# Modulation vectors in whole-vector loads, eight expert weight slots, and a first norm applied after the transpose, in a two-layer hybrid MoE step

## The chip, the cores and the metric

The kernel runs on one core of one Trainium2 chip. Five engines work side by side, each with its own instruction queue: TensorE (PE: matmuls, and transposes done as matmuls), VectorE (DVE), ScalarE (ACT), GpSimd (POOL) and SyncE (SP), which here does nothing but issue DMAs. Semaphores, written out by hand, order them. The metric is the device time of one execution in microseconds; lower is better. All data are FP32.

## The reference

A step of a two-layer backbone (D = 1024), run for 128 prompt tokens with the conditioning `c_ctx` and for 256 latent tokens with `c`:

```python
def modulation(cvec, w_mod_l, b_mod_l):
    m = jax.nn.silu(cvec) @ w_mod_l + b_mod_l
    return m.reshape(cvec.shape[0], 6, D_MODEL)

def trunk_layer(x, mod, ...):
    sh1, sc1, g1, sh2, sc2, g2 = [mod[:, i][:, None, :] for i in range(6)]
    h = rms_norm(x, n1) * (1.0 + sc1) + sh1
    proj = h @ w_in
    q, k, v, u = jnp.split(proj, [Q_W, Q_W + KV_W, Q_W + 2 * KV_W], axis=-1)
    ...                                   # QK-norm, rotary (latent only), softmax attention
    conv = conv_module(u, dw_w, dw_b, ln_g, ln_b)      # 31-tap depthwise convolution
    x = x + g1 * (jnp.concatenate([attn, conv], axis=-1) @ w_out)
    h2 = rms_norm(x, n2) * (1.0 + sc2) + sh2
    x = x + g2 * grouped_moe(h2, w_router, b_router, wg, wu, wd)
    return x, k, v
```

`grouped_moe` sends each token to 2 of 16 experts. An expert is `silu(t @ w_gate) * (t @ w_up)` and then `@ w_down`, each matrix 1024 x 512 or 512 x 1024, 2.1 MB. The weights of a layer (101 MB in the experts, 25 MB for modulation, 11.5 MB in the projections) are read once.

## The kernel before

The 384 tokens are three tiles of 128 (tile 0 the prompt, tiles 1 and 2 the latents), and both conditionings run together: the two cond vectors stand side by side in `cs_rep`, and every modulation product gives rows for both. Tokens stay in `x`.

**Weights.** `ring` has six slots (`SLOTS`) of 16 KB per partition, one per 2.1 MB matrix. Loads are numbered items; item n uses slot n % 6, and SyncE issues them strictly in order, each waiting for `slot_used` of the item six before. A modulation vector of 1024 columns is two items, chunks of 512 columns (`MODC` = 12 chunks a layer, vectors 0 to 5: shift, scale, gate of the first half, then of the second). The order in a layer is: chunks 4 and 5, the four parts of `w_in`, chunks 6 to 9, the two halves of `w_out`, chunks 10 and 11, the next layer's chunks 0 to 3, and then the experts, `g1 u1 d0 g2 u2 d1` and so on. In layer 0 chunks 0 to 3 come first of all.

**Modulation** (`modulation`, line 1277). For a chunk with lanes, TensorE keeps 64 columns of weights (`cs_rep[:, k]`, the two vectors repeated) on each half of the array: the left half streams columns 0 to 255 of the chunk, the right half columns 256 to 511, both at once (line 1294). Chunks 8 and 9, the fifth vector, have no lanes: two columns of weights and 512 streamed (line 1291). VectorE adds the bias (`mod_take`, line 854); for a scale vector it also forms (1 + scale) times the norm's gain. The rows then go to DRAM and come back spread over all partitions (`lane_out` and `spread` on GpSimd) into `shiftB`, `scaleB`, `gateB`. The first ones, of layer 0, are broadcast by TensorE instead (line 1313) and copied out by ScalarE and VectorE.

**Before the experts.** ScalarE squares and sums each tile, GpSimd forms the reciprocal root, and VectorE makes `h` in two passes over 1024 columns (`norm`, lines 907 and 909). TensorE transposes `h` (line 1333), ScalarE copies to `hT`, and 12 projections follow in the order `PROJ` (line 1272). VectorE runs the 31 convolution taps (line 943) between its other duties: the prompt's during the projections; for the latents 6 beside the rotary work, 4 (16 instructions) before the first head, and 3 (12 instructions) in each of the first seven heads. TensorE's modulation work is filler: chunks 6 and 7 around the transposes of q and k, and a quarter of chunk 8 or 9 in each of the 8 heads (`HEAD_FILL`). In a head, VectorE finds the row maxima (line 1023), ScalarE the exponentials, TensorE transposes them, starts the next head's scores, runs the filler and multiplies with v. Then come the output projection (line 1482), the second norm, the router, VectorE's selection, and chunks 10, 11 and the next layer's 0 to 3 as filler.

**Experts** (`expert`, line 1601). GpSimd gathers 128 rows, 64 for each of two experts. TensorE transposes them (line 1552), then per expert: gate and up (line 1568, 16 products of 512 columns on array halves), the down product of the expert before (line 1584), transposes of the hidden rows. An expert with more than 64 tokens has further passes through `overflow`, with their own gather, gate/up and down. `slot_used` of gate and up is raised by tiny products at the very end of the expert (line 1598). At the end of a layer GpSimd gathers the stored expert rows, and `combine` adds them to `x`.

## Time and profile before

| | us |
|---|---|
| median of 3 runs | 1209.04 |
| lowest, highest | 1206.81, 1209.96 |
| the profiled execution | 1206.56 |
| its span, first to last instruction | 1204.7 |

| engine | busy us | share of the span |
|---|---|---|
| TensorE | 995.3 | 83% |
| VectorE | 417.0 | 35% |
| ScalarE | 158.1 | 13% |
| GpSimd | 118.8 | 10% |

The core moves 333.79 MB, 277 GB/s over the span. In the profile the engines are PE, DVE, ACT, POOL and SP; PEld is TensorE's weight load, which overlaps, and a name with q (SPq) is an engine's queue. Each FP32 product that isn't a transpose leaves two records, so "x32" is 16 products. The granted clock of TensorE is a share of 2.4 GHz; 0.5 is the lower of its two levels. The stages of the execution, in us: layer 0 before its experts 0 to 312, its experts 312 to 595, layer 1 before its experts 595 to 875, its experts 875 to 1178, the last combine to the end.

### The profile page before, as it was taken

The numbers are of one execution on the slowest core, as the hardware profiler recorded it, in microseconds if no ns is written. First come the engines' busy times: TensorE is split into PE (matmuls) and PEld (weight loads), VectorE is DVE, ScalarE is ACT, GpSimd is POOL, SyncE is SP. The second block draws the span as 40 slices with busy tenths as digits, with TensorE's granted clock in tenths as the row PEclk, the third lists the DMA queues.
The fourth block names the chain that finished last, engine by engine and source line by source line (L and its number), as shares of the span: only waits on it lengthen the run. The fifth ranks groups of instructions, "written<-read, shape, count | busy, mean of one in ns | idle before, by whom it ended". The sixth has DMA issues, their size and how long they took to land.

```text
span 1204.7 us, 11958 instructions
## 1 busy us (share of the span) xinstructions
PE 995.3 (83%) x4410; PEld 465.3 (39%) x4410; DVE 417.0 (35%) x1070; ACT 158.1 (13%) x354; POOL 118.8 (10%) x164
## 2 busy tenths in 40 slices
PE   3799989998879988888819998999688788788891
PEld 2544545556323333333314554555432223323330
DVE  0229879445111111111051987934410111101113
ACT  0110134220000000000021014422000000000001
POOL 0010300511100000000031030051110000000001
PEclk8899979998889999988858997999688889988996
DMA  9984971387899777999985442135666997999825
GB/s 298 390 294 155 229 267 70 101 241 301 349 420 423 304 308 284 427 426 425 402 299 178 140 159 91 35 122 208 256 237 245 424 424 298 399 427 425 341 88 174
DMA packets 78410, 333.79 MB, mean 277 GB/s; under 512 B 6461, under 2 KB 10685, under 8 KB 61925
## 3 DMA queue, kind: packets, MB, share of 16 engines
q1 hardware_dynamic: 56528, 277.89, 58.2%
q0 software_dynamic: 9104, 30.79, 7.2%
q10 hardware_dynamic: 12676, 23.76, 6.8%
q8 instruction: 64, 1.05, 0.3%
q14 instruction: 38, 0.30, 0.1%
HBM read 310.31 MB, written 22.10 MB: 276 GB/s over the span
## 4 chain that ended last, share of the span: by engine, by line
PE 59%; DMA 22%; DVE 11%; SPq 3%; issue 2%; ACT 2%; POOL 1%; ACTq 0%; DVEq 0%; POOLq 0%
PE ps L1568 17%; PE ps L1272 15%; DMA ring<-in_w_up_dram 14%; PE ps L1584 8%; PE ps L1482 7%; DVE scr L943 4%; DMA ring<-in_w_down_dram 4%; PE ps L1294 3%; DMA scr<-h_rows,slot_tok 2%; PE ps L1407 2%; PE ps L1552 2%; DMA ring<-in_w_mod_dram 2%; SPq L364 1%; DMA scr<-expert_rows,pick_y 1%; PE ps L1291 1%
## 5 line engine op out<-in xcount | busy, mean ns | idle before, releaser
L1568 PE MATMUL ps<-ring,hT 128*64 128x512 f32 x1024 | 257.5, 661 | 52.6 <-DMA ring<-in_w_up_dram 40.3
L1568 PEld LDWEIGHTS ps<-ring,hT 128*64 128x64 f32 x1024 | 83.9, 152 | 201.6 <-issue 187.7
L943 DVE SCALAR_TENSOR_TENSOR scr<-scr,convw 128x128 f32<-128x128 f32 (+1 forms) x480 | 160.7, 415 | 0.0
L1584 PE MATMUL ps<-ring,scr 128*64 128x512 f32 x624 | 144.7, 605 | 5.8 <-DVE scr L1235 3.0
L1272 PE MATMUL ps<-ring,hT 128*128 128x512 f32 (+1 forms) x384 | 147.5, 545 | 0.0
L1244 DVE TENSOR_TENSOR scr<-ps,scr 128x256 f32<-128x256 f32 x32 | 13.6, 425 | 351.3 <-ACT scr L831 351.3
L1294 PE MATMUL ps<-ring,cs_rep 128*64 128x256 f32 x640 | 91.5, 447 | 25.9 <-DMA ring<-in_w_mod_dram 25.9
L1272 PEld LDWEIGHTS ps<-ring,hT 128*128 128x128 f32 x384 | 73.4, 192 | 70.7 <-issue 68.4
L1482 PE MATMUL ps<-ring,hT 128*128 128x512 f32 x192 | 84.4, 594 | 1.3 <-ACT hT L698 1.3
L1584 PEld LDWEIGHTS ps<-ring,scr 128*64 128x64 f32 x624 | 48.8, 139 | 89.8 <-issue 85.4
L1294 PEld LDWEIGHTS ps<-ring,cs_rep 128*64 128x64 f32 x640 | 51.6, 161 | 60.7 <-issue 26.6
L831 ACT ACTIVATE scr<-ps 128x256 f32<-128x256 f32 x32 | 12.3, 383 | 400.0 <-PE ps L1568 400.0
L1568 PE MATMUL ps<-ring,scr 128*64 128x512 f32 x224 | 53.0, 629 | 5.9 <-DVE scr L1224 5.9
L1482 PEld LDWEIGHTS ps<-ring,hT 128*128 128x128 f32 x192 | 35.7, 190 | 43.0 <-issue 41.1
L565 POOL DMA_INDIRECT scr<-h_rows,slot_tok x16 | 15.5, 967 | 317.2 <-PE ps L1552 272.9
L1333 PE MATMUL ps<-table_sb,h 128*128 128x128 f32 x96 | 17.6, 341 | 29.4 <-DVE h L909 29.4
L1216 DVE COPY hT<-ps 128x512 f32<-128x512 f32 x32 | 20.6, 686 | 56.8 <-PE ps L1552 56.8
L1407 PE MATMUL ps<-scr 64*128 64x384 f32 (+1 forms) x96 | 39.4, 500 | 0.0
L1291 PE MATMUL ps<-ring,cs_rep 128*2 128x512 f32 x64 | 32.6, 636 | 0.0
L1552 PE MATMUL ps<-table_sb,scr 128*128 128x128 f32 x128 | 20.1, 305 | 14.8 <-DMA scr<-h_rows,slot_tok 14.8
L1272 PEld LDWEIGHTS ps<-scr 128*128 128x128 f32 x224 | 26.2, 191 | 15.2 <-issue 13.0
L799 ACT COPY scr<-ps 128x512 f32<-128x512 f32 x32 | 18.7, 585 | 100.4 <-PE ps L1584 100.4
(196 smaller groups left out, 770.2 us busy)
## 6 DMA issues: line engine op xcount, KB each, us to landing
ring<-in_w_gate_dram SPq DMA_DIRECT2D x32, 2048.0 KB, 11.5
ring<-in_w_up_dram SPq DMA_DIRECT2D x32, 2048.0 KB, 16.2
ring<-in_w_down_dram SPq DMA_DIRECT2D x32, 2048.0 KB, 20.9
ring<-in_w_mod_dram SPq DMA_DIRECT2D x22, 2048.0 KB, 8.8
ring<-in_w_in_dram SPq DMA_DIRECT2D x6, 2048.0 KB, 19.7
expert_rows<-scr ACTq DMA_DIRECT2D x78, 128.0 KB, 7.6
ring<-in_w_out_dram SPq DMA_DIRECT2D x4, 2048.0 KB, 14.8
expert_rows<-x ACTq DMA_DIRECT2D x1, 6656.0 KB, 36.3
```

The lines of the kernel that those rows point to most:

```text
L799: a.copy(ybuf[:, j, :], ps[:, YB + j, :]).then_inc(y_taken, 1)
L943: v.scalar_tensor_tensor(out, span, w, out, ALU.mult, ALU.add).then_inc(conv_step[part_], 1)
L1216: ins = v.tensor_copy(hT[:, i % 2, 4 * b:4 * b + 4, :].rearrange("p k n -> p (k n)"), ps[:, XT + b, :])
L1272: mm = pe.matmul(out, stationary(k), moving(k), start=(k == 0), stop=(k == n - 1))
L1291: mm = pe.matmul(ps[0:2, mod_bank(l, c), :], cs_rep[:, k, 0:2], w, start=(k == 0), stop=(k == KD - 1))
L1294: mm = pe.matmul(ps[b * LP:(b + 1) * LP, mod_bank(l, c), 0:LW], cs_rep[:, k, :], w[:, b * LW:(b + 1) * LW], start=(k == 0), stop=(k == KD ...
L1333: mm = pe.transpose(ps[:, n % 4, m * P:(m + 1) * P], h[:, t, k::KD], ident)
L1407: pe.matmul(ps[:, 4 + t, 0:P * len(ks)], qT[g_ * HD:(g_ + 1) * HD, t, j * P:(j + 1) * P], kT[g_ * HD:(g_ + 1) * HD, ks[0] * P:(ks[-1] + 1) ...
L1482: mm = pe.matmul(ps[:, out_bank(t, n), :], hT[:, t, k, :], slot_w(s)[:, k, :], start=(k == 0), stop=(k == KD - 1))
L1552: mm = pe.transpose(ps[:, XT + m // 4, m % 4 * P:(m % 4 + 1) * P], xs[:, i % 2, m::KD], ident)
L1568: mm = pe.matmul(ps[b * TT:(b + 1) * TT, bank, :].rearrange("p (m n) -> p m n", m=2), tokens(k), w[:, :, k, b * HF:(b + 1) * HF], start=(k ...
L1584: mm = pe.matmul(ps[b * TT:(b + 1) * TT, bank, :], src[:, k % 2 * P + k // 2 * TT:k % 2 * P + (k // 2 + 1) * TT], w[:, k, b * SEG:(b + 1) ...
```

## The change

**Vectors, not chunks.** An item is now half of a vector's contraction rows, all 1024 columns (4 KB runs in DRAM in place of 2 KB). The left half of the array streams columns 0 to 511, the right half columns 512 to 1023. The fifth vector is done so too. One `mod_take` takes a whole vector, so it needs the vector's last product. In layer 0 the third vector moves from before the projections to behind them. A head's filler is one contraction row of vector 4 (2 products of 512 columns, one on each array half).

**Eight places.** `place()` assigns slots ahead of time by running the order of releases through a list of free slots. Slots 6 and 7 are new for the experts only: slot 6 is the memory of `shiftB` and `scaleB`, free when the second norm is done, slot 7 that of `h` and one tile of `hT`, free when `h` is stored and the router has read. SyncE's loop over the experts is written out.

**The first norm.** VectorE writes only a diagonal matrix with the tile's reciprocal roots (`scale_tile`). TensorE multiplies `x` with it, which scales and transposes at once. ScalarE and VectorE apply scale and shift on the way out of PSUM, four 128-column blocks each per tile, from `modcol`, in which scale and shift are columns. These come through DRAM (`columns`): on ScalarE's queue for layer 0, on GpSimd's for layer 1. The broadcast by TensorE, the copies and the first `spread` pair of layer 1 are gone.

```diff
+def loads(l):
+
+    vec = [("v", l, j, b) for j in range(6) for b in range(2)]
+    proj, out = [("in", l, m) for m in range(4)], [("out", l, n) for n in range(2)]
+    if l == 0:
+        items = vec[0:4] + proj + vec[4:10] + out + vec[10:12]
+    else:
+        items = vec[4:6] + proj + vec[6:10] + out + vec[10:12]
+    if l + 1 < LAYERS:
+        items += [("v", l + 1, j, b) for j in range(2) for b in range(2)]
+    experts = [("g", l, 0), ("u", l, 0)]
+    for e in range(1, E):
+        experts += [("g", l, e), ("u", l, e), ("d", l, e - 1)]
+    return items, experts + [("d", l, E - 1)]
...
+def place():
...
+        at = next((n for n, s in enumerate(free) if s < limit), None)
+        while at is None:
+            done = order.pop(0)
+            free.extend((SLOTS, SLOTS + 1) if done == "norm" else (slot[done],))
+            at = next((n for n, s in enumerate(free) if s < limit), None)
+        slot[item] = free.pop(at)
+        count[slot[item]] += 1
+        use[item] = count[slot[item]]
...
         gateB = sb("gateB", [P, 2, D])
-        h = sb("h", [P, TILES, D])
-        hT = sb("hT", [P, TILES, KD, P])
+        h = ring[:, SLOTS + 1, 0:TILES * D].rearrange("p (t n) -> p t n", n=D)
+        at_hT = ((SLOTS + 1) * KD * SEG + TILES * D)
+        hT = [big[:, at_hT + t * D:at_hT + (t + 1) * D].rearrange("p (k n) -> p k n", k=KD) for t in (2, 1, 0)]
...
+        diag = h[:, :, 0:P]
...
+        def columns(eng, l):
+
+            eng.wait_ge(mod_done, 2 * l + 1)
+            lane_out(eng, mod_dram[:, 0:2 * D], rowA, modA_st[l])
+            eng.wait_ge(modA_st[l], 32)
+            for g_ in range(2):
+                eng.dma_start(modcol[:, g_], mod_dram[g_, 0:2 * D].rearrange("(s p k) -> p s k", s=2, k=KD))\
+                    .then_inc(modcol_in[l], 16)
+
...
-                    load_mod(l, c_)
+                if l:
+                    load_vector(l, 2)
 
                 for m, (c0, n) in enumerate(((QW + 2 * KVW + CH, CH), (QW + 2 * KVW, CH), (0, QW), (QW, 2 * KVW))):
                     if l and m == 2:
                         sp.wait_ge(combined, (l - 1) * TILES + 2)
-                    load(IN_AT[l] + m, w_in_v[l, :, :, c0:c0 + n], n)
-                for c_ in range(MODN, MOD2):
-                    load_mod(l, c_)
+                    load(("in", l, m), w_in_v[l, :, :, c0:c0 + n], n)
+                for j in (2, 3, 4) if l == 0 else (3, 4):
+                    load_vector(l, j)
...
+                def slot_free(n):
+
...
+                    if s >= SLOTS and uses(n) - 1 == (BORROWED[l - 1] if l else 0):
+                        if s == SLOTS:
+                            sp.wait_ge(h_ready, l * 3 + 3)
+                        else:
+                            sp.wait_ge(h2_st, (l + 1) * (TILES * 16))
+                            sp.wait_ge(logit_ps, l * 3 + 3)
+                    elif past(uses(n) - 1):
+                        sp.wait_ge(slot_used[s], uses(n) - 1)
+                    return s
...
                 if l == 0:
-
-                    for n in range(4):
-                        act.wait_ge(first_bc_ps, n + 1)
-                        a.copy(scaleB[:, n // 2, n % 2 * SEG:(n % 2 + 1) * SEG], ps[:, 4 + (n + 1) % 4, :]).then_inc(first_scale, 1)
-                for t in range(TILES):
-                    take_hT(0, t)
+                    columns(act, 0)
+                act.wait_ge(modcol_in[l], 32)
+                for t in range(TILES):
+                    act.wait_ge(hT_ps, l * 18 + 2 * t + 1)
+                    for m in range(4):
+                        ins = a.activation(hT[t][:, m, :], ps[:, 2 * t % 4, m * P:(m + 1) * P], ACT.Identity,
+                                           bias=modcol[:, group(t), 0, m:m + 1], scale=modcol[:, group(t), 1, m:m + 1])
+                    ins.then_inc(hTa_ready, 1)
...
+                def scale_tile(t):
+
+                    dve.wait_ge(rstd_ready, l * 6 + t + 1)
+                    v.tensor_scalar(diag[:, t, :], ident, stats(R1 + t), None, ALU.mult).then_inc(diag_ready, 1)
+
+                def take_hT(t):
+
+                    dve.wait_ge(modcol_in[l], 32)
+                    dve.wait_ge(hT_ps, l * 18 + 2 * t + 2)
+                    for m in range(4):
+                        k = 4 + m
+                        ins = v.tensor_scalar(hT[t][:, k, :], ps[:, (2 * t + 1) % 4, m * P:(m + 1) * P],
+                                              modcol[:, group(t), 1, k:k + 1], modcol[:, group(t), 0, k:k + 1],
+                                              ALU.mult, ALU.add)
+                    ins.then_inc(hTd_ready, 1)
...
+                    scale_tile(0)
                     combine(l - 1, 2)
-                norm(0, 1)
-                norm(0, 2)
+                else:
+                    scale_tile(0)
+                scale_tile(1)
+                scale_tile(2)
                 if l == 0:
-                    mod_take(l, MOD1 + 1)
+                    mod_take(0, 1)
+                for t in range(TILES):
...
+                if l == 0:
+                    mod_take(l, 2)
+                mod_take(l, 3)
                 for k in range(LATE_TAPS):
                     tap(1, ROPE_TAPS + k)
...
-                    if HEAD_FILL[hd][2] == KD:
-                        mod_take(l, HEAD_FILL[hd][0])
+                    if hd == HEADS - 1:
+                        mod_take(l, 4)
...
+            def vector(l, j, k0=0, k1=KD):
+
+                for n, a, b in pieces(l, j):
...
+                        w = slot_k(slot_of(n), b - a)[:, k - a, :]
+                        for lane in range(LANES):
+                            mm = pe.matmul(ps[lane * LP:(lane + 1) * LP, mod_bank(l, j), :], cs_rep[:, k, :],
+                                           w[:, lane * LW:(lane + 1) * LW], start=(k == 0), stop=(k == KD - 1))
+                        if k == b - 1:
+                            mm.then_inc(slot_used[slot_of(n)], 1)
...
+                for t in range(TILES):
+                    pe.wait_ge(diag_ready, l * 3 + t + 1)
+                    if t == 2:
+                        hT_first(0)
+                    for n in range(2 * t, 2 * t + 2):
+                        for m in range(4):
+                            mm = pe.matmul(ps[:, n % 4, m * P:(m + 1) * P], x[:, t, 4 * (n % 2) + m::KD], diag[:, t, :],
+                                           start=True, stop=True)
+                        mm.then_inc(hT_ps, 1)
 
...
-                modulation(l, MODN, 0, KD // 2)
+                if l == 0:
+                    vector(l, 2)
+                vector(l, 3, 0, 2)
...
                     if t == 2:
                         mm.then_inc(qkT_ps, 1)
-                    c, k0 = ((MODN, KD // 2), (MODN + 1, 0), (MODN + 1, KD // 2))[t]
-                    modulation(l, c, k0, k0 + KD // 2)
+                    vector(l, 3, 2 * t + 2, 2 * t + 4)
...
-                    c, k0, k1 = HEAD_FILL[hd]
-                    if k0 == 0 and c > 8:
-                        pe.wait_ge(mod_taken, l * MODC + c)
-                    modulation(l, c, k0, k1)
+                    if hd == 0:
+                        pe.wait_ge(mod_taken, taken_at(l, 3))
+                    vector(l, 4, hd, hd + 1)
```

On TensorE, in layer 0 between the last projection and the first head (1395 or 1421 are the transposes of q and k), before:

```order
L1272 MATMUL ps<-ring,hT 128x256 x8
L1294 MATMUL ps<-ring,cs_rep 64x256 x8
L1391 MATMUL ps<-table_sb,scr 128x128
L1395 MATMUL ps<-table_sb,h 128x128 x4
L1397 MATMUL ps<-table_sb,scr 128x128
L1294 MATMUL ps<-ring,cs_rep 64x256 x8
```

and in the changed kernel:

```order
L1314 MATMUL ps<-big 128x256 x8
L1330 MATMUL ps<-big,cs_rep 64x512 x20
L1417 MATMUL ps<-table_sb,scr 128x128
L1421 MATMUL ps<-table_sb,big 128x128 x4
L1423 MATMUL ps<-table_sb,scr 128x128
L1330 MATMUL ps<-big,cs_rep 64x512 x4
```

16 products of 512 columns, the third vector, and the fourth's first four now stand ahead of the transposes. On VectorE, from the end of the last tile's rotary work to the maxima of the first head, before:

```order
L1008 TENSOR_TENSOR scr<-scr 128x128
L872 TENSOR_TENSOR scaleB<-ps,scaleB 128x256
L943 SCALAR_TENSOR_TENSOR scr<-scr,convw 128x256 x16
L872 TENSOR_TENSOR scaleB<-ps,scaleB 128x256
L1023 TENSOR_REDUCE stat<-ps 128x1 x3
```

and in the changed kernel (`big` is the memory of the slots, here the fourth vector's row):

```order
L1052 TENSOR_TENSOR scr<-scr 128x128
L906 TENSOR_TENSOR rowC<-ps,rowC 128x512
L906 TENSOR_TENSOR big<-ps,big 128x512
L987 SCALAR_TENSOR_TENSOR scr<-scr,convw 128x256 x16
L1068 TENSOR_REDUCE stat<-ps 128x1 x3
```

The second take moved from behind the 16 taps to ahead of them. On SyncE, with the semaphore that each issue waits for, from layer 0's first expert load, before (the last rows are in a loop):

```order
L413 DMA ring<-in_w_gate_dram 128x4096 [waits slot_used4]
L413 DMA ring<-in_w_up_dram 128x4096 [waits slot_used5]
L413 DMA ring<-in_w_gate_dram 128x4096 [waits slot_used0]
L413 DMA ring<-in_w_up_dram 128x4096 [waits slot_used1]
L421 DMA ring<-in_w_down_dram 128x2x2048 [waits slot_used2]
```

and in the changed kernel:

```order
L462 DMA big<-in_w_gate_dram 128x4096 [waits h_ready]
L462 DMA big<-in_w_up_dram 128x4096 [waits logit_ps,h2_st]
L462 DMA big<-in_w_gate_dram 128x4096 [waits slot_used4]
L462 DMA big<-in_w_up_dram 128x4096 [waits slot_used5]
L467 DMA big<-in_w_down_dram 128x2x2048 [waits slot_used0]
L462 DMA big<-in_w_gate_dram 128x4096 [waits slot_used1]
L462 DMA big<-in_w_up_dram 128x4096 [waits slot_used2]
L467 DMA big<-in_w_down_dram 128x2x2048 [waits slot_used3]
```

The first expert's two matrices no longer wait for the slots of chunks 10 and 11, and each later load of this stage stands two slots earlier in the course of the filler.

## Rows read from the trace of the kernel before

**Rows 1.** The page, part 4: shares of the span by line in the chain.
```profile
PE ps L1568 17%; PE ps L1272 15%; DMA ring<-in_w_up_dram 14%; PE ps L1584 8%; PE ps L1482 7%; DVE scr L943 4%; DMA ring<-in_w_down_dram 4%; PE ps L1294 3%; DMA scr<-h_rows,slot_tok 2%; PE ps L1407 2%; PE ps L1552 2%; DMA ring<-in_w_mod_dram 2%; SPq L364 1%; DMA scr<-expert_rows,pick_y 1%; PE ps L1291 1%
```

**Rows 2.** Windows: start:end length, engines' busy us (instructions), TensorE clock, DMA share, GB/s.
```profile
312.50:595.20 282.70, 238.98 (x1102) 90.94 (x1104) 34.57 (x74) 17.82 (x37) 10.82 (x13) 0.92 0.92 376
875.40:1178.00 302.60, 254.30 (x1160) 94.55 (x1160) 36.44 (x78) 18.78 (x39) 9.49 (x10) 0.91 0.81 330
390.00:480.00 90.00, 79.36 (x378) 30.14 (x374) 12.60 (x27) 6.78 (x14) 2.81 (x3) 0.96 0.74 299
870.00:930.00 60.00, 48.31 (x226) 19.25 (x228) 8.18 (x17) 3.29 (x7) 3.69 (x4) 0.90 0.62 229
930.00:990.00 60.00, 50.53 (x226) 18.29 (x223) 7.49 (x16) 3.87 (x8) 2.81 (x3) 0.88 1.01 426
990.00:1050.00 60.00, 49.98 (x242) 19.73 (x242) 6.74 (x15) 3.87 (x8) 0.97 (x2) 0.94 0.84 348
```

**Rows 3.** Waits of the whole span: who waited for whom, us, times, longest.
```profile
PE ps L1568 <- DMA ring<-in_w_up_dram: 40.3, 13, 6.8
...
PE ps L1598 <- issue: 18.0, 6, 4.0
```

**Rows 4.** Timeline of TensorE, experts: start, us, instructions, idle time before and its releaser.
```profile
354.84 9.97 PE L1568 MATMUL ps<-ring,hT 128*64 128x512 f32 x32 [6.77 <-DMA ring<-in_w_up_dram]
...
455.18 7.09 PE L1568 MATMUL ps<-ring,scr 128*64 128x512 f32 x32 [0.93 <-DVE scr L1224]
...
1102.85 9.73 PE L1568 MATMUL ps<-ring,hT 128*64 128x512 f32 x32 [0.54 <-DMA ring<-in_w_up_dram]
```

**Rows 5.** Timeline of the SyncE queue, third expert's loads in layer 0.
```profile
311.21 0.35 SPq L413 DMA_DIRECT2D ring<-in_w_gate_dram  x1
321.70 0.34 SPq L413 DMA_DIRECT2D ring<-in_w_up_dram  x1
```

**Rows 6.** Heads of layer 0: window of one head, then its modulation products.
```profile
184.86:191.54 6.68, 6.68 (x34) 3.46 (x33) 6.41 (x19) 2.81 (x9) 0.00 (x0) 1.00 0.03 3
...
188.12 1.88 PE L1291 MATMUL ps<-ring,cs_rep 128*2 128x512 f32 x4
```

**Rows 7.** Timeline of TensorE at the start of layer 0.
```profile
30.72 3.67 PE L1294 MATMUL ps<-ring,cs_rep 128*64 128x256 f32 x32 [0.43 <-DMA ring<-in_w_mod_dram]
36.39 5.36 PE L1294 MATMUL ps<-ring,cs_rep 128*64 128x256 f32 x32 [2.00 <-DMA ring<-in_w_mod_dram]
...
67.58 12.61 PE L1272 MATMUL ps<-ring,hT 128*128 128x512 f32 x29
```

**Rows 8.** Timeline around the entry to layer 0's heads.
```profile
141.93 1.95 PE L1294 MATMUL ps<-ring,cs_rep 128*64 128x256 f32 x16
...
151.69 0.66 PE L1395 MATMUL ps<-table_sb,h 128*128 128x128 f32 x4 [2.56 <-DVE scr L1008]
151.89 6.42 DVE L943 SCALAR_TENSOR_TENSOR scr<-scr,convw 128x256 f32<-128x256 f32 x16
...
152.39 3.63 PE L1294 MATMUL ps<-ring,cs_rep 128*64 128x256 f32 x16
...
158.55 1.22 DVE L1023 TENSOR_REDUCE stat<-ps 128x1 f32<-128x128 f32 x3
```

**Rows 9.** DMA issues (KB each, median us to landing), and a timeline row.
```profile
scr<-in_b_mod_dram ACTq DMA_DIRECT2D x4, 256.0 KB, 8.2
...
mod_rows<-rowC POOLq DMA_DIRECT2D x4, 4.0 KB, 5.5
...
310.06 0.75 POOL L472 DMA_DIRECT2D gateB<-mod_rows  x1 [14.27 <-DMA mod_rows<-scaleB]
```

**Rows 10.** Timeline of the first norm of layer 1.
```profile
622.43 1.28 DVE L907 SCALAR_TENSOR_TENSOR h<-x,stat,scaleB 128x1024 f32<-128x1024 f32 x1 [0.74 <-POOL stat L468]
...
623.75 1.23 DVE L909 TENSOR_TENSOR h<-h,shiftB 128x1024 f32<-128x1024 f32 x1
...
634.46 1.97 PE L1333 MATMUL ps<-table_sb,h 128*128 128x128 f32 x8 [1.29 <-DVE h L909]
```

467 lines of the change are left out of this document (201 added, 266 removed).

## The prediction

> **What bounds the kernel now.** I read the page first: the chain of work that ended last is mostly TensorE matmuls, led by the experts' gate and up products (line 1568), but `w_up` transfers hold a large second share [rows 1]. So I asked for the stages. The reader is to see in the windows of the two expert phases that TensorE is busy for 239 of 283 us and for 254 of 303 us, and that the DMA engines run in two regimes: 426 GB/s where they are full, and 299, 229 and 348 GB/s where they are not [rows 2]. Both engines idle, in turn, in one phase: the signature of a buffer that is too short. The waits say how much of it TensorE pays, both layers together: 40.3 us for `w_up`, and 18.0 us of stops at the small products that end an expert [rows 3]. The timeline shows the cause. The 16 gate/up products of an expert take 7.09 us. After 6.77 us of waiting the same products take 9.97 us, because the granted clock has dropped, so a wait costs up to 2.9 us more than itself; there are eleven such slow sets, the last at 1102.85. An expert with more than 64 tokens runs everything twice (such a second pass starts at 455.18), another 7.1 us and a down product during which its slots stay occupied [rows 4]. The SyncE queue shows the other side: `g2` leaves at 311.21, `u2` only at 321.70, when expert 0 has finished [rows 5]. Six slots are two experts of lookahead.
>
> Before the experts, each layer is bound by TensorE or by short chains; the loads of layer 0's first two vectors bound the first 50 us.
>
> **The change part by part.** All times are against the profiled execution, 1206.56 us with a span of 1204.7; the median of the three runs shown is 1209.04, 2.5 us higher.
>
> *Eight places for expert weights.* A 2.097 MB load takes 4.92 us at 426 GB/s [rows 2], so two more places hold 9.8 us of transfer per stretch in which the DMA would otherwise stop. The placement lets gate and up of an expert wait for the expert three back, not two, and lets `g0` go as soon as the second norm is done.
> - Layer 0: the gap is 90 us at 299 GB/s, or 90 x (1 - 299/426) = 26.8 us of DMA idleness, spread over three experts with a second pass, 8.9 us each, under the 9.8 that two places cover. The last experts still wait a little, since transfers (some 5.4 us per load with the row stores and gathers beside it) are slower than a plain expert's 12 us per three loads. I take -24.
> - Layer 1: 60 us at 229 GB/s is 27.7 us idle, 60 us at 348 is 11.0. The first gap is the ring standing full before expert 0 and during expert 1's second pass: two places fill 9.8, and one more load of 4.9 can go in the second pass because `d2` no longer queues behind `g3`. The second gap gives its 9.8. Sum -24.5. The two experts with second passes at the end are TensorE's own time and stay.
> - Bounds: TensorE can't get back more than it loses. In both layers that is 40.3 + 18.0 us of waits and 27.0 us that the eleven slow sets took above 7.09 each, 85.3 in all [rows 3, 4]; at the other end it gets nothing.
>
> *The heads' fifth vector on column halves.* Two products of 512 columns with 2-column weights take 1.88 us a head [rows 6]; as two halves side by side they should take half, since a chunk of 16 products with 256 columns takes 3.67 us [rows 7], which is 4 x 0.92. So TensorE falls from 6.68 to 5.74 us a head. But VectorE is busy 6.41 us of those 6.68 [rows 6]: the gain in a middle head is at most 0.27 us, 1.7 over six heads, not 5.6. The first head runs at half clock and is TensorE's, so it gives 1.6.
>
> The Trainium skill, page "TensorEngine Tiling (Array Packing)", Key Properties, says that changing the tiling mode drains TensorE, which speaks against putting half-array products between full-array ones in each head. The trace shows 8 products of that kind ahead of full-array work in 1.95 us, against 3.67 for 16 in a row [rows 7, 8]: at most 0.12 us for the switch. With it or without it, VectorE hides it; the sum is the same.
>
> *What VectorE now waits for.* This is the part that costs. Before, the fourth vector was taken in two chunks: the first was ready when the rotary work ended, then 16 taps ran (6.42 us), and the second chunk had arrived under them [rows 8]. Now `mod_take(l, 3)` stands ahead of the taps and needs the whole vector, whose last quarter TensorE computes after the transposes of tile 2, which wait for the same rotary work. Behind it on VectorE are 16 taps and then the first head's maxima, for which ScalarE and TensorE wait. In layer 1: transposes 0.76, fill 3.6 at half clock, take 0.7, taps 6.42, so the maxima come 11.5 us after the rotary end instead of 6.9: +4.6 (+2.8 at full clock). In layer 0 the third vector (7.3 us) is put in front too. TensorE starts its fills at 141.93, then 7.3 + 1.8, and three times transposes 0.9 and fill 1.8: 159.1. Take, taps: maxima at 166.3, not 158.55 [rows 8]: +7.7. From this come off head 0 (1.6), the middle heads (1.7) and about 2 us that TensorE had as slack behind the last tap. Net +3 in layer 0, 0 in layer 1; range 0 to +7.7 and -2 to +4.6.
>
> *Start of layer 0.* Removed: the broadcast products, the copies and two passes of the norm; and the fifth and sixth chunk move behind the projections. Added: a trip through DRAM, mod row out and column in, then the affine on the way out of PSUM. The second vector is complete at about 41.8, as before: its last products start at 36.39 and take 5.36 us [rows 7], but VectorE first scales three diagonals, so the row is done at 46. Two small stores with weights streaming beside them took 5.5 us; a store of the same sort took 14.3 in the worst wait [rows 9]. Reading 512 pieces of 32 bytes is not in the trace; the nearest are 8.2 us for 64 x 4 pieces of 1 KB per transfer, and 5.5 for a few rows. I take 8.2. With some 2 us for four issues: columns at 62. Then tile 0's affine (1.1), tile 2's products, which wait for tile 0's banks (3.4 at half clock), and the first projection at 66.5 instead of 67.58 [rows 7]; 1.2 lost to the clock leaves 0. From -5 (both trips at 5.5 us) to +9 (a 14.3 us store).
>
> *First norm of layer 1.* Here the columns are there long before. VectorE's two passes (1.28 + 1.22) become one pass over 128 columns, an eighth of the width and about 0.2 us [rows 10]. Ahead of tile 2's products lie tile 0's and tile 2's passes: -4.6. The products with a diagonal are true FP32 products: 3.4 us for 8 at half clock against 1.97 for transposes [rows 10]: +1.4. Net -3.2. The `w_mod` and `w_in` loads behind the last expert now trail it more closely while the pick-up gathers run: +1 (0 to +5).
>
> Nothing for: the unrolled SyncE loop (its issues take 0.3 us each, between waits of 10 us [rows 5]), SBUF moves, fewer and longer `w_mod` rows.
>
> Sum: -24 - 24.5 + 3 + 0 + 0 - 3.2 + 1 = -47.7. That is 1158.9 against the profiled run, 1161.3 against the median; I give 1160.
>
> **The rivals.**
> - *Half the gain.* The places help only once per layer, when they are first filled, and afterwards transfers set the pace: 2 x 9.8. For it: between 930 and 990 the DMA is full (426 GB/s) and TensorE still idles 9.5 of 60 us [rows 2]. Against: each second pass empties the DMA anew. 1206.6 - 19.6 + 0.8 = 1187.8.
> - *The bytes bind.* If the 376 GB/s mean of layer 0's phase were all that memory gives, no place would help: 1206.6 + 0.8 = 1207.4. A window of 60 us at 426 speaks against [rows 2]. The Trainium skill, "DMA: Bandwidth & Descriptors", Specifications, gives about 358 GB/s of HBM per core, by which this would be the case; the trace disagrees with it by those rows.
> - *Slower.* VectorE's wait for the whole fourth vector is paid in full (7.7 + 4.6), because the heads are in step with VectorE and give nothing back: +12.3 - 3.2 + 1 = +10.1. It decides only where the expert phases give back less than that; with nothing from them 1216.7.
> - *The heads follow TensorE.* If VectorE's 6.41 us were waiting in disguise, six heads in two layers would give 12 x 0.66 = 8 more: 1151. Against: 12 taps alone are 4.8 us of work.
> - *All waits go*: 85.3 in place of 48.5: 1122. Against: transfers are slower than plain experts.
>
> **How the numbers follow.** Forecast 0.63, half the gain 0.14, heads 0.10, all waits 0.05, bytes 0.04, slower 0.04. The forecast's own ends are about 1142 and 1180 (phases at 18 to 32 us each, the start at -5 to +9). The range 1138 to 1190 takes in the halved gain and the faster heads and leaves out the last three cases and tails, 0.2 together. A measurement of this kernel tells 0.3%, 3.6 us, from no change: faster 0.92, within it 0.04, slower 0.04.
>
> **What would show it.** Right: expert phases of about 259 and 278 us with waits for `w_up` mostly gone until the last four experts; no window under 380 GB/s in the middle of layer 0's phase; heads of 6.4 us with VectorE busy throughout; an idle stretch of VectorE ahead of its take of vector 3, 7 us in layer 0; the first projection at 66 +- 3 us. Wrong: maxima of head 0 that come no later, column reads that land in 3 or in 20 us, or expert waits that move to `w_down`.

## The result: 1.0% slower, with most stages near the forecast and the heads far from it

| | before | after |
|---|---|---|
| median, us | 1207.92 (4 runs, 1201.93 to 1209.96) | 1218.95 (4 runs, 1218.12 to 1220.15) |
| the profiled execution | 1206.56 | 1218.12 |
| its span | 1204.7 | 1216.3 |
| ratio after / before | | 1.0103, 95% interval 1.0075 to 1.0132 |

The forecast was 1160 us, with a range of 1138 to 1190 and a chance of 0.92 for faster. Sign and range are both wrong.

**Where the time went.** Windows of the changed kernel (columns as in [rows 2]): head 0 of layer 0; all heads of layer 0 and of layer 1; the expert stretches of layer 0 and of layer 1.

```profile
165.00:176.00 11.00, 11.00 (x32) 6.12 (x32) 5.00 (x13) 3.77 (x13) 0.00 (x0) 0.50 1.04 353
165.00:247.50 82.50, 82.50 (x243) 46.43 (x244) 46.50 (x119) 21.92 (x70) 1.18 (x3) 0.50 0.32 114
740.50:821.30 80.80, 80.78 (x243) 44.98 (x244) 46.53 (x119) 21.95 (x70) 0.00 (x0) 0.51 0.12 40
344.90:606.40 261.50, 233.53 (x1102) 89.01 (x1104) 34.56 (x74) 17.85 (x37) 11.24 (x13) 0.95 0.95 389
908.20:1189.70 281.50, 245.04 (x1160) 94.24 (x1160) 36.43 (x78) 18.82 (x39) 9.49 (x10) 0.96 0.83 340
```

The expert stretches answer to the first two lines of [rows 2]: 282.7 and 302.6 us are now 261.5 and 281.5 (in the table below the first is 282.8, ending at 595.3 and not 595.2). The heads are what the prediction hardly looked at. Here are the same stretches of the kernel before, head 0 first, then all heads of layer 0 and of layer 1:

```profile
160.70:171.50 10.80, 10.77 (x32) 4.64 (x32) 5.04 (x13) 3.80 (x13) 0.00 (x0) 0.59 1.04 384
160.70:216.10 55.40, 55.20 (x242) 27.95 (x243) 46.45 (x121) 22.11 (x70) 0.05 (x1) 0.92 0.33 117
731.30:786.40 55.10, 54.92 (x243) 27.93 (x244) 46.39 (x121) 22.04 (x70) 0.07 (x1) 0.92 0.08 24
```

The reader is to compare two columns. VectorE's busy time is the same (46.4 against 46.5 us). TensorE's granted clock is 0.92 before and 0.50 after: all eight heads of layer 0, and those of layer 1 but for the end of the last, now run at the lower of the two levels, 1.2 GHz, and the heads take 27.1 us more in layer 0 and 25.7 in layer 1. In both kernels the first head starts at the lower clock. In the kernel before it ends at the higher one. These are the rows of TensorE in head 0 of layer 0, first of the kernel before: its first transpose, its fill products, and its products of the weights with the values.

```profile
160.73 0.47 PE L1431 MATMUL ps<-table_sb,scr 128*128 128x128 f32 x1 [3.00 <-ACT scr L754]
...
166.67 3.29 PE L1291 MATMUL ps<-ring,cs_rep 128*2 128x512 f32 x4
169.89 1.77 PE L1272 MATMUL ps<-scr 128*128 128x64 f32 x14
```

The same three of the changed kernel:

```profile
164.99 0.48 PE L1456 MATMUL ps<-table_sb,scr 128*128 128x128 f32 x1 [7.52 <-ACT scr L791]
...
170.93 1.98 PE L1330 MATMUL ps<-big,cs_rep 128*64 128x512 f32 x4
172.84 3.25 PE L1314 MATMUL ps<-scr 128*128 128x64 f32 x14
```

Before, two long products run one behind the other for 3.29 us, the clock rises under them, and the seven value products behind them (14 records) take 1.77 us. After, the two halves run side by side for 1.98 us, nothing rises, and the value products take 3.25 us; so they do in each head after it. A head is 10.8 us instead of 6.68 [rows 6].

One head is different. In the last head of layer 1, which has no scores of a next head between its transposes, the clock does rise under the single pair, and the value products are short again:

```profile
816.41 1.70 PE L1456 MATMUL ps<-table_sb,scr 128*128 128x128 f32 x7
818.04 1.71 PE L1330 MATMUL ps<-big,cs_rep 128*64 128x512 f32 x4
819.68 1.77 PE L1314 MATMUL ps<-scr 128*128 128x64 f32 x14
```

In layer 0's last head it does not (value products 3.25 us). So what is said below of a single pair holds for the first seven heads of a layer.

The second difference is TensorE's idle time in front, 7.52 us instead of 3.00. Which of the two matters is what the experiments have to say.

**The whole balance**, layer by layer, between the two profiled executions:

| stretch | before | after | difference |
|---|---|---|---|
| start to head 0, layer 0 | 160.7 | 165.0 | +4.3 |
| heads, layer 0 | 55.4 | 82.5 | +27.1 |
| heads to experts | 96.4 | 97.4 | +1.0 |
| experts, layer 0 | 282.8 | 261.5 | -21.3 |
| experts to head 0 of layer 1 | 136.0 | 134.1 | -1.9 |
| heads, layer 1 | 55.1 | 80.8 | +25.7 |
| heads to experts | 89.0 | 86.9 | -2.1 |
| experts, layer 1 | 302.6 | 281.5 | -21.1 |
| the end | 26.7 | 26.6 | -0.1 |
| sum | 1204.7 | 1216.3 | +11.6 |

### The profile page after: what moved, and what is told of

Same layout as the page of the kernel before. It is cut to its first block, busy times and chain, and to the rows that moved or that the text cites. A ratio compares the mean times of both kernels' runs of the same rounds, so it can differ in the third digit from the quotient of the medians.

```text
span 1216.3 us, 11203 instructions
## 1 busy us (share of the span) xinstructions
PE 1034.2 (85%) x4106; PEld 480.6 (40%) x4106; DVE 406.9 (33%) x1068; ACT 157.8 (13%) x362; POOL 120.4 (10%) x170
## 4 chain that ended last, share of the span: by engine, by line
PE 70%; DMA 16%; DVE 5%; issue 2%; POOL 2%; ACT 2%; SPq 1%; DVEq 0%; ACTq 0%; POOLq 0%
PE ps L1590 19%; PE ps L1314 17%; DMA big<-in_w_up_dram 10%; PE ps L1606 9%; PE ps L1330 6%; PE ps L1506 6%; PE ps L1432 4%; PE ps L1456 2%; DMA x<-in_x_sample_dram 2%; DMA scr<-h_rows,slot_tok 1%; PE ps L1367 1%; PE ps L1574 1%; DMA scr<-expert_rows,pick_y 1%; DVE scr L987 1%; PE ps L1599 1%
## 5 line engine op out<-in xcount | busy, mean ns | idle before, releaser
L1590 PE MATMUL ps<-big 128*64 128x512 f32 x1024 | 243.6, 626 | 40.9 <-DMA big<-in_w_up_dram 21.0
L1606 PE MATMUL ps<-big,scr 128*64 128x512 f32 x624 | 147.9, 611 | 4.6 <-DVE scr L1277 4.3
L1590 PEld LDWEIGHTS ps<-big 128*64 128x64 f32 x1024 | 81.1, 143 | 178.8 <-issue 166.9
L1314 PE MATMUL ps<-big 128*128 128x512 f32 (+1 forms) x384 | 145.5, 539 | 0.0
L1330 PE MATMUL ps<-big,cs_rep 128*64 128x512 f32 x384 | 117.0, 749 | 19.6 <-DMA big<-in_w_mod_dram 19.4
L1314 PEld LDWEIGHTS ps<-big 128*128 128x128 f32 x384 | 72.7, 191 | 69.4 <-issue 67.0
L1506 PE MATMUL ps<-big 128*128 128x512 f32 x192 | 84.4, 594 | 1.3 <-ACT big L735 1.3
L1606 PEld LDWEIGHTS ps<-big,scr 128*64 128x64 f32 x624 | 50.1, 141 | 89.4 <-issue 88.1
L1330 PEld LDWEIGHTS ps<-big,cs_rep 128*64 128x64 f32 x384 | 28.8, 164 | 85.7 <-issue 69.7
L869 ACT ACTIVATE scr<-ps 128x256 f32<-128x256 f32 x32 | 12.3, 384 | 356.5 <-PE ps L1590 356.5
L1590 PE MATMUL ps<-big,scr 128*64 128x512 f32 x224 | 51.3, 612 | 5.9 <-DVE scr L1266 5.9
L1506 PEld LDWEIGHTS ps<-big 128*128 128x128 f32 x192 | 35.7, 190 | 43.0 <-issue 41.1
L1314 PE MATMUL ps<-scr 128*128 128x64 f32 x224 | 50.5, 416 | 0.0
```

Source lines behind the costliest of these rows:

```text
L1314: mm = pe.matmul(out, stationary(k), moving(k), start=(k == 0), stop=(k == n - 1))
L1330: mm = pe.matmul(ps[lane * LP:(lane + 1) * LP, mod_bank(l, j), :], cs_rep[:, k, :], w[:, lane * LW:(lane + 1) * LW], start=(k == 0), stop= ...
L1506: mm = pe.matmul(ps[:, out_bank(t, n), :], hT[t][:, k, :], slot_w(s)[:, k, :], start=(k == 0), stop=(k == KD - 1))
L1590: mm = pe.matmul(ps[b * TT:(b + 1) * TT, bank, :].rearrange("p (m n) -> p m n", m=2), tokens(k), w[:, :, k, b * HF:(b + 1) * HF], start=(k ...
L1606: mm = pe.matmul(ps[b * TT:(b + 1) * TT, bank, :], src[:, k % 2 * P + k // 2 * TT:k % 2 * P + (k // 2 + 1) * TT], w[:, k, b * SEG:(b + 1) ...
```

## The experiments

The theory after the comparison: the fifth vector on column halves keeps TensorE at the lower clock through the heads. Rival 1: the longer idle time ahead of head 0 does it. In the fences below, windows are of layer 0's and layer 1's heads where nothing else is said.

**e1_lanes: this part alone, on the kernel before.**

```
 def lanes(c):
-    return c not in (8, 9)
+    return True
...
-pool.dma_start(rowS, b_mod[l:l + 1, 4 * D:5 * D].broadcast_to([2, D])).then_inc(rowB_in, 16)
+lane_in(pool, rowS, b_mod[l:l + 1, 4 * D:5 * D], rowB_in)
```

> The kernel before with one part of the change alone: the fifth modulation vector on column halves (its row, gain and store with it); six weight places, the old first norm and the old half-vector items stay. Theory (the filler on column halves keeps TensorE at the lower clock): the granted clock of the heads is 0.50 in both layers instead of 0.94, a head takes about 10.8 us as in the changed kernel, the heads 80 us a layer instead of 55, and the time is about 1208 + 50 = 1258 us. Rival 1 (TensorE's longer idle time ahead of head 0, 7.5 us instead of 3.0, keeps the clock low): that idle time is 3.0 us here as before, so the clock rises in head 0, a head takes 6.4 to 6.7 us and the time is 1205 to 1210 us. Rival 2 (memory places, banks or the new norm are at fault): as rival 1.

Measured: 1267.43 us, ratio 1.0495 (1.0456 to 1.0534).

```profile
162.50:244.90 82.40, 82.40 (x274) 50.17 (x275) 46.60 (x121) 21.88 (x70) 1.72 (x4) 0.50 0.25 90
762.10:842.70 80.60, 80.60 (x275) 48.76 (x275) 46.67 (x121) 21.92 (x70) 0.32 (x1) 0.51 0.06 17
```

The part alone costs 5%. TensorE's idle time ahead of head 0 is as before in layer 0 (3.05 us); in layer 1 it is 4.68 us against 3.05. The heads take the changed kernel's times to 0.2 us. Eight places, whole-vector items and the new first norm are not needed for it. The total is 60 us up, not 50; 52 of them are in the heads.

**e4_idle: the idle time alone, on the kernel before.**

```
+for _ in range(11):
+    step.link(v.tensor_reduce(stats(NM), ps[:, 4, 0:P * len(KEY_CHUNKS[0])], AX.X, ALU.max, negate=True))
 score_max(0)
```

> The kernel before with eleven more small reductions on VectorE ahead of head 0's maxima in each layer, so that TensorE's idle time ahead of head 0 is about 7.5 us instead of 3.0, as in the changed kernel. Theory (column halves): the clock rises in head 0 all the same, heads stay 55 us a layer, and only the delay is paid: 1208 + 2 x 4.5 = 1217 us. Rival 1 (idle time ahead of head 0): the granted clock of the heads falls to 0.50, a head takes 11 to 12 us, and the time is 1208 + 9 + 50 = 1267 us or more.

Measured: 1218.14 us, ratio 1.0092 (1.0058 to 1.0127): only the delay is paid, so rival 1 falls. In layer 1 the idle time was 8.25 us, more than the changed kernel's 7.52, and the clock rose in head 0. Layer 0's head 0 and head 1, and then head 0 of layer 1, show that there is some chance in it:

```profile
165.32 0.48 PE L1435 MATMUL ps<-table_sb,scr 128*128 128x128 f32 x1 [6.68 <-ACT scr L754]
...
171.26 3.57 PE L1295 MATMUL ps<-ring,cs_rep 128*2 128x512 f32 x4
174.77 3.25 PE L1276 MATMUL ps<-scr 128*128 128x64 f32 x14
...
183.69 3.40 PE L1295 MATMUL ps<-ring,cs_rep 128*2 128x512 f32 x4
187.02 1.78 PE L1276 MATMUL ps<-scr 128*128 128x64 f32 x14
...
743.43 0.47 PE L1435 MATMUL ps<-table_sb,scr 128*128 128x128 f32 x1 [8.25 <-ACT scr L754]
...
752.88 2.01 PE L1276 MATMUL ps<-scr 128*128 128x64 f32 x14
```

In layer 0, 3.57 us of long products did not raise the clock (the value products behind them take 3.25), and it rose one head later, under the same products (3.40, and then value products in 1.78). Layer 0's heads took 61.3 us, layer 1's 55.9.

**e2_apart: the two halves apart within each head, on the changed kernel.** Lane 0's product where both were, lane 1's behind the value products.

```
-vector(l, 4, hd, hd + 1)
+vector(l, 4, hd, hd + 1, (0,))
...
 mm.then_inc(o_ps, 1)
+vector(l, 4, hd, hd + 1, (1,))
```

> The changed kernel with the two column halves of the fifth vector taken apart in each head: the first half's product stands where both stood, the second half's product behind the products of the weights with the values. Same products, same output. Theory (overlap of the two products keeps TensorE below what raises the clock): the clock rises in head 0 of each layer, heads take 6.6 to 6.9 us each, 55 to 57 us a layer instead of 83 and 77, and the time is about 1219 - 47 = 1172 us. Rival 1 (idle time ahead of head 0): the 7.5 us of idle time stay, the clock stays at 0.50, and each head is about 1.7 us longer than 10.8, since nothing overlaps: 1219 + 16 x 1.7 = 1246 us.

Measured: 1251.21 us, ratio 1.0364 (1.0329 to 1.0398). The rise that my theory wanted did not come, and the time is near the rival's 1246.

```profile
166.70:263.60 96.90, 96.86 (x243) 47.89 (x243) 45.19 (x117) 21.93 (x70) 0.00 (x0) 0.51 0.25 91
```

```profile
172.68 1.97 PE L1330 MATMUL ps<-big,cs_rep 128*64 128x512 f32 x2
174.58 3.25 PE L1314 MATMUL ps<-scr 128*128 128x64 f32 x14
177.76 1.97 PE L1330 MATMUL ps<-big,cs_rep 128*64 128x512 f32 x2
```

The head has as much long work as in the kernel before, in two pieces of 1.97 us, and the clock stays down until the last head (0.50 from 166.7 to 260, then it rises). With e4 having cleared the idle time, the theory has to be put otherwise: not that the halves overlap, but that the unbroken piece of long products became short.

**e3_wake: a longer piece in head 0 alone, on the changed kernel.** Two more pairs, results overwritten, in head 0 of each layer.

```
+for _ in range(0 if hd else 2):
+    for lane in range(LANES):
+        pe.matmul(ps[lane * LP:(lane + 1) * LP, mod_bank(l, 4), :], cs_rep[:, 0, :],
+                  slot_k(...)[:, 0, lane * LW:(lane + 1) * LW], start=True, stop=True)
 vector(l, 4, hd, hd + 1)
```

> The changed kernel with two more pairs of column-half products ahead of the filler of head 0 in each layer, whose results are overwritten. Theory, first form (the clock only has to be raised once, and the shorter heads hold it): the clock rises in head 0, the other seven heads take 6.4 us, about 1219 - 47 + 3 = 1175 us. Second form (what is in each head decides, however it starts): the clock stays at 0.50 or falls back in head 1 or 2, and the time is 1219 + 2 x 3.6 = 1226 us, less what is won while the clock is up. Rival 1 (idle time ahead of head 0): no statement on the extra products; the clock stays at 0.50, 1226 us.

Measured: 1166.94 us, ratio 0.9667 (0.9617 to 0.9716), 52 us below the changed kernel, with more work. Its head 0, and then the windows of the heads:

```profile
166.97 0.48 PE L1456 MATMUL ps<-table_sb,scr 128*128 128x128 f32 x1 [7.52 <-ACT scr L791]
...
172.91 3.59 PE L1467 MATMUL ps<-big,cs_rep 128*64 128x512 f32 x8
176.33 1.03 PE L1330 MATMUL ps<-big,cs_rep 128*64 128x512 f32 x4
177.29 1.77 PE L1314 MATMUL ps<-scr 128*128 128x64 f32 x14
```

```profile
167.00:222.20 55.20, 51.60 (x250) 29.04 (x251) 44.96 (x119) 22.28 (x70) 0.69 (x2) 0.90 0.51 184
718.90:774.30 55.40, 51.76 (x251) 28.81 (x252) 45.03 (x119) 22.36 (x70) 0.33 (x1) 0.90 0.18 62
```

The idle time is still 7.52 us. After 3.59 us of pairs in one piece the next pair takes 1.03 us instead of 1.98, and seven heads with a single pair each hold the higher clock. The added pairs are column halves too, so it isn't this kind of product that keeps the clock down. The heads of the changed kernel can hold the clock; the first seven can't raise it. This is the first form of the theory, some 8 us better than the 1175 it had put.

**e9_lump: the same without added work.** The eight pairs of a layer are spread otherwise: two in head 0, one in each of heads 1 to 6, none in head 7.

```
-vector(l, 4, hd, hd + 1)
+vector(l, 4, hd + 1 if hd else 0, min(hd + 2, KD))
```

> The changed kernel with the fifth vector's eight pairs spread otherwise: head 0 takes the first two pairs in one piece, heads 1 to 6 take one each, head 7 none. The same products and the same output, nothing added. Theory (at the lower clock one unbroken piece of long products raises the clock, a single pair of 1.9 us does not, and once raised the heads hold it): the clock rises in head 0, the heads take 53 to 54 us a layer instead of 82.5 and 80.8, and the time is 1219 - 57 = 1162 us. Rival (it needs more than two pairs, or it needed the extra work): 0.50 through the heads, 1219 us.

Measured: 1173.58 us, ratio 0.9717 (0.9677 to 0.9757). In the profiled execution (1164.0 us, as expected) the clock rose in head 0 of both layers (x8 is two pairs; layer 0's heads took 55.3 us, layer 1's 55.7):

```profile
170.96 3.68 PE L1330 MATMUL ps<-big,cs_rep 128*64 128x512 f32 x8
174.57 1.88 PE L1314 MATMUL ps<-scr 128*128 128x64 f32 x14
```

The other three executions took 1173 to 1175 us at a lower mean clock (0.906 to 0.914 against 0.922). A rise one head later, as in e4, would fit them, but they have no profile, so this is not shown. A different order of the same products is worth 45 us.

**e5_gap: nothing in the heads, the idle time filled.** Seventeen dummy products ahead of head 0.

```
 for t in range(TILES):
     scores(0, t)
+for _ in range(17):
+    pe.matmul(ps[:, 2, :], ident, x[:, 0, 0:SEG], start=True, stop=True)
```

> The changed kernel with seventeen dummy 128x512 products (results overwritten) put into TensorE's 7.5 us of idle time ahead of head 0 in each layer; nothing is added inside the heads. Theory as the run with two more pairs left it (the clock falls in that idle time, 162 to 164 us there, and the short filler of the heads can hold the clock but not raise it): with the idle time filled the clock stays at 1.00, head 0 takes 6.6 us instead of the 11.9 of that run, and the time is 1167 - 2 x 5.3 = 1156 us. Rival (only a run of long products within a head raises the clock, whatever is ahead of it): the clock is 0.50 through the heads and the time is 1219 us as for the changed kernel.

Measured: 1162.87 us, ratio 0.9620 (0.9601 to 0.9639). The fill and the heads of layer 0, and the heads of layer 1:

```profile
157.73 14.86 PE L1450 MATMUL ps<-x,table_sb 128*128 128x512 f32 x34
```

```profile
172.40:222.00 49.60, 46.01 (x243) 27.36 (x242) 41.37 (x109) 21.35 (x66) 1.11 (x3) 0.98 0.43 160
720.90:769.60 48.70, 45.11 (x244) 26.49 (x243) 41.37 (x109) 21.36 (x66) 0.23 (x1) 1.00 0.20 68
```

The clock never falls, head 0 is as fast as the others, and all eight take 49 us, 6.2 each. I had priced a dummy at half of what it takes (14.86 / 17 = 0.87 us), so head 0 begins at 172.4, 5.4 us later than in e3, and gives back what it gains: 1163, not 1156.

**e6_taps_gap: the stall in front of head 0 taken away as well.**

```
-mod_take(l, 3)
 for k in range(LATE_TAPS):
     tap(1, ROPE_TAPS + k)
+mod_take(l, 3)
```

and four dummy products instead of seventeen.

> The changed kernel with VectorE's take of the fourth vector moved behind the four late taps (they run in VectorE's 6.4 us of idle time), so that head 0's maxima and TensorE's first transpose come some 6 us earlier, and four dummy 128x512 products ahead of head 0 for what is left of TensorE's idle time. Theory: the clock stays at 1.00 into the heads, as in the run with seventeen products, and 2 x 5.9 us more are won: about 1156 - 12 = 1144 us. Rival (VectorE bounds the stretch and the taps only change places): the same as with seventeen products, 1156 us. If the idle time left is long enough for the clock to fall, the heads stay at 0.50: 1219 - 12 = 1207 us.

Measured: 1145.11 us, ratio 0.9471 (0.9445 to 0.9497), as expected.

```profile
163.20:212.40 49.20, 45.60 (x243) 27.03 (x242) 43.08 (x114) 21.35 (x66) 0.78 (x2) 0.98 0.65 236
702.80:752.40 49.60, 46.01 (x243) 27.47 (x243) 44.85 (x119) 22.38 (x70) 1.12 (x3) 0.98 0.31 110
```

This kernel, the changed one with one line moved and one loop added, is the best of all: 5.3% below the kernel before, and 0.9471 / 1.0103 = 0.937 of the changed one.

**e12_fit: the dummies fitted to the idle time** (`range(5 if l else 1)`).

> The run with the take behind the taps and dummy products, with their number fitted to the idle time: one in layer 0 (1.3 us idle), five in layer 1 (4.7 us idle), at the 0.93 us that one took at full clock. Theory: the clock stays at 1.00 in both layers and no product delays head 0: 1145 - 2 = 1142 to 1143 us. Rival (the delay of the surplus products in layer 0 was hidden by VectorE): 1145 us.

Measured: 1148.76 us, ratio 0.9533 (0.9507 to 0.9560). No gain over e6: the two profiled spans are equal (1146.9 and 1146.6), as the rival had it: the surplus was hidden.

**e10_taps: the line moved, no dummies.**

> The changed kernel with VectorE's take of the fourth vector moved behind the four late taps, and no dummy products: the order of the two alone. TensorE's idle time ahead of head 0 becomes about 1.3 us in layer 0 and 4.7 in layer 1 (from the run with four products, less those). Theory: after 1.3 us the clock is still 1.00 and layer 0's heads take 49 us; in layer 1 it falls within the 4.7 us and the heads stay at 0.50, 80 us: 1145 - 2 + 31 = 1174 us. Rival (any idle time, or its lack of dummy work, loses the clock): both layers at 0.50, 1207 us.

Measured: a median of 1202.85 us in four executions, against 1174 expected. The profiled one took 1179.86 us and does what was expected: layer 0's heads hold the clock after 1.18 us of idle time, in layer 1 it falls while TensorE idles for 4.62 us (second line) and stays down.

```profile
160.50:210.10 49.60, 45.96 (x243) 27.43 (x243) 45.30 (x120) 22.42 (x70) 1.22 (x4) 0.98 0.70 258
695.00:697.00 2.00, 0.00 (x0) 0.00 (x0) 2.00 (x6) 0.00 (x0) 0.00 (x0) 0.74 1.06 410
699.40:780.00 80.60, 80.59 (x242) 44.99 (x243) 46.52 (x119) 21.89 (x70) 0.00 (x0) 0.51 0.15 50
```

Its other three executions took 1202 to 1209 us at a mean clock of 0.868 to 0.876 (0.897 in the profiled one): 23 to 29 us more, near the 31 us by which the heads of the two layers differ here. That layer 0's heads ran at the lower clock too in these three would fit, but they have no profile. The same kernel on the same data has two outcomes.

**e11_taps_lump: both order edits, no dummies.**

> Both of the last two edits together: the take behind the late taps, and two pairs in head 0. No work is added. Theory: layer 0's heads run at 1.00 from the start (49 us), layer 1's head 0 begins at 0.50 and raises the clock (53 us): 1145 - 2 + 4 = 1147 us. Rival (one of the two edits spoils the other): 1160 us or more.

Measured: 1158.12 us, ratio 0.9599 (one execution of four took 1185.75, at 0.894 against 0.915 to 0.918). The heads of the two layers took 54.0 and 55.1 us, against 49 and 53 expected. Layer 0's first head begins after the same 1.18 us of idle time as in e10, and here the clock falls:

```profile
156.50:158.30 1.80, 0.64 (x2) 0.02 (x1) 1.69 (x4) 1.78 (x4) 1.49 (x3) 1.00 1.04 393
158.30:165.00 6.70, 6.68 (x17) 2.76 (x19) 5.40 (x14) 4.00 (x13) 0.00 (x0) 0.58 1.05 369
```

So the length of the idle time alone doesn't tell whether the clock falls; two products in one piece then raised it again.

**e7_six: the eight places undone, on e3.** The experts' loads get six places; the rest of the change stays.

```
 for item in experts:
-    take(item, MOE_SLOTS)
+    take(item, SLOTS)
```

> The run with two more pairs in head 0 (1167 us), with the experts' loads kept to six places instead of eight; all else stays. Theory (the eight places are worth what the expert stretches of the two traces show, 21 us in each layer): 1167 + 42 = 1209 us, the expert stretches 283 and 303 us. Rival (the places are worth nothing, the other parts of the change gave it): 1167 us.

Measured: 1197.41 us, ratio 0.9910 (0.9892 to 0.9929). The expert stretches:

```profile
318.60:593.40 274.80, 235.60 (x1102) 92.33 (x1104) 34.52 (x74) 17.81 (x37) 11.18 (x13) 0.94 0.93 379
871.70:1168.70 297.00, 254.97 (x1160) 97.38 (x1160) 36.39 (x78) 18.78 (x39) 9.45 (x10) 0.92 0.83 336
```

The two places are worth 1197.4 - 1166.9 = 30.5 us, not the 42 that the stretches gained. About 8 us of layer 0's stretch and 6 of layer 1's are gained with six places already, by something else in the change (the placement of items, or the order of loads). Both are outside what the six-place kernels before wander over (282.7 to 288.1 and 302.6 to 308.4). Which part it is was not tried.

**e8_lanes_wake, e13_before_gap, e14_lanes_gap: what the fifth vector's part is worth without the clock.** e8 is e1 with four more pairs of 256 columns in head 0. e13 is the kernel before, and e14 is e1, each with three of e5's dummies ahead of head 0.

> The kernel before with the fifth vector on column halves (1267 us) and four more pairs of 128x256 products ahead of head 0's filler in each layer, whose results are overwritten. Theory (the whole loss of that part is the clock): the clock rises in head 0 and holds, heads 1 to 7 take 6.4 us, and the time is that of the kernel before with the price of the longer head 0, 1207 - 2 + 2 x 2.3 = 1210 us. Rival (the column halves cost in another way too): anything from 1215 us up.

> The kernel before with three dummy 128x512 products in TensorE's 3.0 us of idle time ahead of head 0 in each layer. Theory (the clock falls in that idle time in the kernel before too, and head 0 pays it): the clock stays at 1.00, head 0 takes 6.7 us instead of 10.8, the heads 51 us a layer instead of 55.4, and the time is about 1206 - 8 = 1198 us. Rival (head 0 is slow for another reason, as its own first steps): no change, 1204 to 1208 us.

> The kernel before with the fifth vector on column halves and the same three dummy products ahead of head 0. Theory A (the prediction's term is right once the clock is held, -0.27 us in each middle head): 2 to 4 us below the run without the column halves, about 1195 us. Theory B (what the four-pair run left over is a cost of this part outside the heads, of 9 to 12 us): about 1207 us with heads of 49 to 50 us a layer and the surplus in the expert stretches. Rival (the clock isn't held by these heads in this kernel): 1260 us.

Measured: e8 1219.58 us, ratio 1.0103 (1.0074 to 1.0132), on its rival's side; e13 1199.27 us, ratio 0.9943 (0.9922 to 0.9964), as expected; e14 1205.79 us in 11 executions, which fall in two groups: seven of 1198 to 1207 us at a mean clock of 0.906 to 0.911, with a median of 1202.61, and four of 1231 to 1232 at 0.880 to 0.887. The 29 us between the groups would fit one layer of heads at the lower clock, which no profile shows; e14's ratio without the second group, 0.9983 (0.9962 to 1.0004), is no difference. The heads of e13, then of e14:

```profile
161.60:212.90 51.30, 51.12 (x242) 26.80 (x243) 46.33 (x121) 22.17 (x70) 0.03 (x1) 1.00 0.35 125
730.20:786.20 56.00, 55.82 (x242) 28.36 (x243) 46.40 (x121) 22.05 (x70) 0.04 (x1) 0.91 0.08 24
```

```profile
162.10:211.80 49.70, 45.30 (x274) 28.96 (x275) 45.16 (x121) 22.41 (x70) 0.86 (x2) 0.99 0.45 163
729.80:780.50 50.70, 46.30 (x274) 29.97 (x275) 45.16 (x121) 22.40 (x70) 1.87 (x4) 0.97 0.16 55
```

In layer 0, where both hold the clock, column halves take the heads from 51.3 to 49.7 us: 1.6 us, where the prediction said 1.7 for the middle heads. TensorE is then idle for 4.4 us of them, and VectorE sets the pace, as it was put. In layer 1 e13's heads began at the lower clock and e14's did not, after the same 1.9 us of idle time. But e13's profiled execution is the slowest of its ten (1207.59 us; the others took 1195 to 1202), so its fall in layer 1 and its expert stretches needn't be the rule. Over the whole kernel the part gives nothing that can be told (e14's first group has a median 3 us above e13's, where 2 to 4 us below were expected), and e8 lies 12 us above the kernel before, of which 3.2 are in the heads and some 7 in the expert stretches (284.3 and 308.4 us). These stretches wander by as much with six places and no column halves (282.7 and 305.2 in e4, 288.1 and 304.4 in e13), so I can't put it down to the part. It stays open.

## Why the prediction was wrong, step by step

- **Eight places** (said -24 and -24.5): -21.3 and -21.1; waits for `w_up` fell from 40.3 us [rows 3] to 21.0. The size was right to 13%. The attribution was not: by e7, the places are 30.5 us of the 48.5 forecast, and the rest of the 42 is something else in the change. The eleven slow sets behind the bound of 85.3 us were also too few: two more of 8.78 us stand behind the one at 1102.85, at 1131.36 and 1159.30. Only that bound and the rival of all waits use the count.

```profile
PE ps L1590 <- DMA big<-in_w_up_dram: 21.0, 8, 4.2
```

- **Start of layer 0** (said 66.5 for the first projection): 64.6, three us before the 67.58 of [rows 7]. The way through DRAM took 45.57 to 59.04, from the store's issue to the first use of the columns, 13.5 us where two hops at 8.2 and 5.5 plus four issues had been put at 16. Tile 2's eight products with the diagonal took 4.17 us at the lower clock, not 3.4.

```profile
45.57 0.59 ACTq L289 DMA_DIRECT2D mod_rows<-scr  x2
...
59.04 2.91 ACT L727 ACTIVATE big<-ps,modcol 128x128 f32<-128x128 f32 x8 [16.10 <-DMA modcol<-mod_rows]
...
64.61 2.94 PE L1314 MATMUL ps<-big 128*128 128x512 f32 x6
```

- **VectorE's wait for the whole fourth vector** (said +7.7 in layer 0, with an idle stretch of 7 us ahead of the take): the idle stretch is 6.42 us, and the maxima start at 162.82 instead of 158.55 [rows 8]: +4.3, which with the start's -3.0 is +7.3. The net was added up wrongly: 7.7 less 1.6, 1.7 and 2 is 2.4, not 3, and layer 1's 4.6 less the same is -0.7, not 0. Moving one line takes it away: the maxima start at 164.80 in e3 and at 158.71 in e6.

```profile
155.88 0.69 DVE L906 TENSOR_TENSOR big<-ps,big 128x512 f32<-128x512 f32 x1 [6.42 <-PE ps L1330]
...
162.82 1.21 DVE L1068 TENSOR_REDUCE stat<-ps 128x1 f32<-128x128 f32 x3
```

- **First norm of layer 1** (said -3.2, and +1 for the loads): from the end of layer 0's experts to the first projection it is -2.5 (595.3 to 636.22 before, 606.4 to 644.83 after). Two things more make the table's -1.9. The projections take 2.2 us less, which the prediction didn't have: the products with the diagonal have raised the clock by then (0.50 from 633.2 to 637, 1.00 from 641 to 645), where before it rose under the projections. And from the end of the rotary work to the maxima of head 0 it is 9.8 us instead of 6.9, the +2.8 that was given for the full clock.
- **Loads behind the last expert** (said +1): not visible.
- **The heads** (said -1.6 for head 0 and -1.7 for six middle heads a layer): +27.1 and +25.7. This is the step that failed: "The first head runs at half clock and is TensorE's, so it gives 1.6." I took the clock of head 0 as a fact of the place and the clock 1.00 of a middle head [rows 6] as another, and computed each head at its own clock. I never asked where in between the clock rises, and so put the price of its not rising at nothing. It rises under the two products that the change makes shorter (166.67 above). Had I asked, the rival would have been plain: if it doesn't rise, seven heads a layer stay at the lower clock, and TensorE's 5.74 us a head nearly doubles, past VectorE's 6.41. Fourteen heads that take 10.8 us in place of 6.68 are 58 us; 52.8 were measured (the last head of a layer has less to do, and in layer 1 the clock rises in it).
- The rival called slower (1216.7) came within 3 us of the measured time, and for a wrong reason: its mechanism is VectorE's wait, its price 12.3 us, and it needed expert stretches that give nothing. The wait is real and near its price (7.3 us in layer 0, 2.8 in layer 1), but the stretches give 42 us. What eats them is the clock of the heads, which no rival names. A number that comes out right is no evidence for its mechanism.
- What is left of the forecast is in e5, with the changed kernel's heads at the higher clock and the 6 us stall still there: 1162.87 against 1160. That it comes so close is partly luck: e5 holds the clock in head 0 as well, which the forecast did not have, and begins head 0 later by as much; and by e7 some 14 us of the gain in the expert stretches are not the places.

The Trainium skill, "TensorE: Matmul & The Clock Gate", Part 1, says that the throttled clock is the default and that activity releases it. The trace agrees that it has two levels and falls while TensorE waits (to 0.74 and then 0.50 in e10's layer 1). It disagrees with the simple reading that a busy TensorE gets its clock: in the changed kernel TensorE is shown busy for 82.50 of 82.50 us at 0.50 (layer 0's heads).
